# Loading the projection weights of a decoder layer in pairs of units

## The reference

```python
mod = (silu(c) @ w_ada + b_ada)                    # 2048 x 12288 weights: six parts
h = rmsnorm(x, g_pre_mix) * (1.0 + sc1) + sh1
proj = h @ w_in                                    # 2048 x 6160: q, k, v | GLA q, k, v, r | gate
o_sb = stick_breaking_attention(q, k, v)           # prompt; samples also read 64 cached pages of K and V
o_g  = gated_linear_attention(q_g, k_g, v_g, log_alpha, state) * silu(r_g)
m = concat(norm(o_sb), norm(o_g)) @ w_out          # 2048 x 2048
x = x + gt1 * rmsnorm(m, g_post_mix)
h = rmsnorm(x, g_pre_ffn) * (1.0 + sc2) + sh2
f = (silu(h @ w_ffn_gate) * (h @ w_ffn_up)) @ w_ffn_down
y = x + gt2 * rmsnorm(f, g_post_ffn)
```

## Time and profile before

| | us |
|---|---|
| median of 3 runs | 1502.29 (1501.54 to 1504.39) |
| the profiled execution | 1500.96 |
| its span in the trace | 1499.2 |
| slots 0 to 127 (first unit's matmul to the last) | about 99 to 685 |
| FFN and end | about 707 to 1499 |

### The profile page before, as it was taken

The page is one execution under the profiler, slowest core; times in us unless marked ns, Lnnn a source line. Parts: engine busy times, 40 slices in busy tenths (PEclk is TensorE's granted clock), DMA queues, the critical chain, the costliest instruction groups (busy, mean ns, idle before and its releaser), DMA issues.

```text
span 1499.2 us, 29221 instructions
## 1 busy us (share of the span) xinstructions
PE 1431.8 (96%) x11274; PEld 1272.5 (85%) x11274; DVE 913.4 (61%) x1501; ACT 661.2 (44%) x1277; POOL 105.3 (7%) x205
## 2 busy tenths in 40 slices
PE   6779999999799999998999999999999999999997
PEld 2247787887577787796899999999999999999997
DVE  2143588995777656457656666566665665446444
ACT  1023477777556553336443434434344343334333
POOL 1000311113322200100000000000000000200000
PEclk9979999999999999999999999999999999999999
DMA  9999999999999978987765565655666656855552
GB/s 369 421 341 357 391 392 405 376 333 399 401 381 332 337 261 276 400 317 268 255 187 178 167 194 178 184 177 167 191 181 182 180 170 186 236 181 182 178 179 93
DMA packets 139043, 396.54 MB, mean 265 GB/s; under 512 B 13131, under 2 KB 17394, under 8 KB 126146
## 3 DMA queue, kind: packets, MB, share of 16 engines
q1 hardware_dynamic: 117730, 319.39, 62.6%
q0 software_dynamic: 21232, 76.10, 13.4%
HBM read 382.14 MB, written 11.21 MB: 262 GB/s over the span
## 4 chain that ended last, share of the span: by engine, by line
PE 83%; DMA 10%; DVE 3%; ACT 2%; issue 1%; POOLq 0%; POOL 0%; SPq 0%; DVEq 0%; ACTq 0%
PE ps L1907 24%; PE ps L1908 24%; PE ps L1909 24%; DMA ada_s<-in_w_ada 5%; PE ps L1841 4%; DMA v_page<-in_cache_v 2%; DMA k_page<-in_cache_k 2%; PE ps L2039 2%; PE ps L1965 1%; DMA ada_r<-in_w_ada 1%; ACT k_page L780 0%; DVE k_page L1275 0%; PE ps L2068 0%; ACT w_hi L702 0%; PE ps L2060 0%
## 5 line engine op out<-in xcount | busy, mean ns | idle before, releaser
L1907 PE MATMUL ps<-h_hi,w_hi 128*128 128x264 f32 x2304 | 665.9, 289 | 6.2 <-DVE h_lo L1213 3.6
L1908 PE MATMUL ps<-h_lo,w_hi 128*128 128x264 f32 x2304 | 656.7, 285 | 0.0
L1909 PE MATMUL ps<-h_hi,w_lo 128*128 128x264 f32 x2304 | 656.2, 285 | 0.0
L1907 PEld LDWEIGHTS ps<-h_hi,w_hi 128*128 128x128 f32 x2304 | 436.1, 189 | 51.2 <-issue 36.9
L1729 DVE TENSOR_TENSOR w_lo<-raw,w_hi 128x1024 fp32r<-128x1024 f32 x256 | 309.5, 1214 | 275.5 <-ACT w_hi L1018 274.1
L1018 ACT ACTIVATE w_hi<-raw 128x1024 fp32r<-128x1024 f32 x264 | 278.4, 1059 | 405.0 <-PE ps L1909 391.2
L1908 PEld LDWEIGHTS ps<-h_lo,w_hi 128*128 128x128 f32 x2304 | 435.5, 189 | 0.1
L1909 PEld LDWEIGHTS ps<-h_hi,w_lo 128*128 128x128 f32 x2304 | 434.4, 189 | 0.0
L1225 DVE TENSOR_TENSOR w_lo<-raw,w_hi 128x1024 fp32r<-128x1024 f32 x136 | 166.2, 1223 | 151.1 <-ACT w_hi L702 143.8
L702 ACT ACTIVATE w_hi<-raw 128x1024 fp32r<-128x1024 f32 x128 | 134.9, 1055 | 182.6 <-PE ps L1909 161.8
L1908 PE MATMUL ps<-act_lo,w_hi 128*128 (+1 forms) x704 | 200.4, 285 | 0.0
(11 more groups left out here) (336 smaller groups left out, 1205.5 us busy)
## 6 DMA issues: line engine op xcount, KB each, us to landing
ada_r<-in_w_ada SPq DMA_DIRECT2D x64, 1024.0 KB, 9.5
raw<-in_w_in SPq DMA_DIRECT2D x96, 512.0 KB, 8.9
raw<-in_w_ffn_gate SPq DMA_DIRECT2D x88, 512.0 KB, 3.7
raw<-in_w_ffn_up SPq DMA_DIRECT2D x88, 512.0 KB, 3.9
raw<-in_w_ffn_down SPq DMA_DIRECT2D x88, 512.0 KB, 4.5
ada_s<-in_w_ada SPq DMA_DIRECT2D x32, 1024.0 KB, 13.7
k_page<-in_cache_k POOLq DMA_DIRECT2D x64, 512.0 KB, 8.1
v_page<-in_cache_v POOLq DMA_DIRECT2D x38, 512.0 KB, 8.1
```

What stands on the lines that cost most here:

```text
L1907: mm(out, w_hi, xh, start=first, stop=False)
L1908: mm(out, w_hi, xl, start=False, stop=False)
L1909: return mm(out, w_lo, xh, start=False, stop=last)
```

## The change

Two neighbouring units, an even and an odd one, are loaded by one transfer of 1 MB into two neighbouring places of `RAW`. The pair has one semaphore of two (`pair_in`) in place of one of four; `hi` of either unit waits for the whole pair. The pair (u, u+1) is issued where the odd unit was issued, at the odd slots, once DVE has split unit u - 3; so the even unit's issue moves one slot later, behind the `ada_load` or `state_load` of the even slot. At the start, pairs (0,1) and (2,3) are issued where units 0 to 3 were, and pair (4,5) where unit 5 was. In slot 2 nothing is loaded before the wait for `x_moved`.

Two semaphores more are needed and three are given back: `kft_ready` and `sfin_ready` become counts 1 and 2 of `gla_copied`, and `vs_copied` becomes counts 2 and 3 of `vsmp_ready`, with the same instructions as signallers and the same ones waiting. The bytes moved and the arithmetic are the same.

```diff
--- before.py
+++ after.py
@@ -253,12 +253,12 @@
         W_DOWN = W_FFN + 2 * NFF * UPC
         NSLOT = W_FFN
 
-        def unit_src(u):
+        def pair_src(u):
             g, j = divmod(u, UPC)
             if g < NIN:
-                return win_v[:, 2 * j:2 * j + 2, IN_COL[g]:IN_COL[g] + CG]
+                return win_v[:, 2 * j:2 * j + 4, IN_COL[g]:IN_COL[g] + CG]
             kp = (j + 4) % UPC
-            return wout_v[:, 2 * kp:2 * kp + 2, (g - NIN) * CG:(g - NIN) * CG + CG]
+            return wout_v[:, 2 * kp:2 * kp + 4, (g - NIN) * CG:(g - NIN) * CG + CG]
 
         def unit_dst(g, m):
             return PROJ[:, IN_DST[g] + m, :] if g < NIN else MT_[:, (g - NIN) * MT + m, :]
@@ -305,6 +305,7 @@
 
         c_in, x_in, vec_in, misc_in = sem("c_in"), sem("x_in"), sem("vec_in"), sem("misc_in")
         raw_in = sems("raw_in", 4)
+        pair_in = sems("pair_in", 2)
         ads_in = sems("ads_in", 6)
         ada_in = sems("ada_in", 9)
         kpage_in = sems("kpage_in", 5)
@@ -329,7 +330,7 @@
         k_mul, k_even, k_odd = sem("k_mul"), sem("k_even"), sem("k_odd")
         t_diff, t_exp, t_mul, t_mm, t_mask = sem("t_diff"), sem("t_exp"), sem("t_mul"), sem("t_mm"), sem("t_mask")
         att_cross, pick_ready = sem("att_cross"), sem("pick_ready")
-        kft_tr, kft_ready, g_st, sfin_ready, g_o, g_oev = sem("kft_tr"), sem("kft_ready"), sem("g_st"), sem("sfin_ready"), sem("g_o"), sem("g_oev")
+        kft_tr, gla_copied, g_st, g_o, g_oev = sem("kft_tr"), sem("gla_copied"), sem("g_st"), sem("g_o"), sem("g_oev")
         vg_tr, vg_ready, vsmp_ready = sem("vg_tr"), sem("vg_ready"), sem("vsmp_ready")
         km_ready, qz_ready = sem("km_ready"), sem("qz_ready")
         dec_mm, dec_taken = sem("dec_mm"), sem("dec_taken")
...
@@ -388,7 +389,8 @@
             sp.dma_start(PT[:, :], page_table.rearrange("b n -> (b n)").unsqueeze(0)).then_inc(misc_in, 16)
 
             def w_load(u):
-                sp.dma_start(RAW[:, u % 4, :].rearrange("p (k n) -> p k n", k=2), unit_src(u)).then_inc(raw_in[u % 4], 16)
+                sp.dma_start(RAW[:, u % 4:u % 4 + 2, :].rearrange("p s (k n) -> p (s k) n", k=2), pair_src(u))\
+                    .then_inc(pair_in[u // 2 % 2], 16)
 
             def ada_load(n):
                 p = ADA_PLACE[n]
@@ -399,13 +401,12 @@
             for n in range(6, 2 * KC):
                 sp.wait_ge(ads_used, n - 5)
                 sp.dma_start(ADS[n % 6][:, :], ada_start(n)).then_inc(ads_in[n % 6], 16)
-            for u in range(4):
+            for u in (0, 2):
                 w_load(u)
 
             sp.dma_start(WG[:, :, :], win_v[:, :, NIN * CG:NIN * CG + RANK]).then_inc(misc_in, 16)
-            for u in range(4, 6):
-                sp.wait_ge(lo_ready, u - 3)
-                w_load(u)
+            sp.wait_ge(lo_ready, 2)
+            w_load(4)
 
             sp.wait_ge(ads_used, 2 * KC)
             sp.wait_ge(tr_done, 2 + KC)
@@ -425,7 +426,8 @@
 
             for s in range(2, NSLOT - 4):
                 sp.wait_ge(lo_ready, s + 1)
-                w_load(s + 4)
+                if s % 2:
+                    w_load(s + 3)
                 if s == 2:
                     sp.wait_ge(x_free, 1)
                     sp.wait_ge(x_moved, 16)
...
@@ -696,7 +698,7 @@
                 s.activation((MROW0 if q < 4 else MROW1)[:, :], ps[:, TURN_BANK[q], :], ACT.Copy).then_inc(modrow, 1)
 
             def hi(u):
-                act.wait_ge(raw_in[u % 4], 16 * (u // 4 + 1))
+                act.wait_ge(pair_in[u // 2 % 2], 16 * (u // 4 + 1))
                 if u >= 4:
                     act.wait_ge(unit_used, u - 3)
                 s.activation(HI[:, u % 4, :], RAW[:, u % 4, :], ACT.Copy).then_inc(hi_ready, 1)
...
@@ -1567,7 +1569,7 @@
                     ins.then_inc(norm_sq, 1)
                 if st == 90:
                     dve.wait_ge(bank_out, 44)
-                    v.tensor_copy(VSMP[:, 0:4, :], PV[:, :, TP:T]).then_inc(vs_copied, 1)
+                    v.tensor_copy(VSMP[:, 0:4, :], PV[:, :, TP:T]).then_inc(vsmp_ready, 1)
                 if st == 91:
                     dve.wait_ge(norm_sum, 1)
                     rstd_of(rstd[0:64, :], rvar[0:64, :], ps[0:64, 4, 0:T], 1, 2)
...
```

More of the change, by code:

```diff
@@ L341, in stickbreak_gla_layer @@
         tok_tr, kt_ready, vt_ready = sem("tok_tr"), sem("kt_ready"), sem("vt_ready")
-        row_tr, row_ready, vs_copied = sem("row_tr"), sem("row_ready"), sem("vs_copied")
+        row_tr, row_ready = sem("row_tr"), sem("row_ready")
         norm_sq, norm_sum, norm_rs, norm_bc, norm_h = sem("norm_sq"), sem("norm_sum"), sem("norm_rs"), sem("norm_bc"), sem("norm_h")
@@ L615, in _ @@
                 if s == 56:
-                    pool.wait_ge(sfin_ready, 1)
+                    pool.wait_ge(gla_copied, 2)
                     pool.dma_start(new_state_prompt[0, 0].rearrange("h k v -> k h v"), SFIN[:, :, :]).then_inc(sfin_out, 16)
@@ L728, in evac_frees @@
                     act.wait_ge(tok_tr, 6)
-                    act.wait_ge(vs_copied, 1)
+                    act.wait_ge(vsmp_ready, 2)
                 if g == 12:
@@ L928, in _ @@
                         ins = s.activation(KFT[:, j * 512:j * 512 + 512], ps[:, 5 + j, :], ACT.Copy)
-                    ins.then_inc(kft_ready, 1)
+                    ins.then_inc(gla_copied, 1)
                 if st == 56:
@@ L935, in _ @@
                         ins = s.activation(SFIN[:, 2 * j:2 * j + 2, :].rearrange("p h v -> p (h v)"), ps[:, 5 + j, :], ACT.Copy)
-                    ins.then_inc(sfin_ready, 1)
+                    ins.then_inc(gla_copied, 1)
                 if st in (58, 59):
@@ L1015, in hi_n @@
             def hi_n(nb, u):
-                act.wait_ge(raw_in[u % 4], nb * 4 + (64 // 4 * (u // 4) + 16))
+                act.wait_ge(raw_in[u % 4], nb * 4 + (64 // 4 * (u // 4) + 16 - 4 * W_FFN))
                 act.wait_ge(unit_used, nb + (u - 3))
@@ L1592, in slot @@
                     dve.wait_ge(bank_out, 48)
-                    v.tensor_copy(VSMP[:, 4:8, :], PV[:, :, TP:T]).then_inc(vs_copied, 1)
+                    v.tensor_copy(VSMP[:, 4:8, :], PV[:, :, TP:T]).then_inc(vsmp_ready, 1)
                 if st == 98:
@@ L2080, in gla_values @@
                 if h < 2:
-                    pe.wait_ge(sfin_ready, 1)
+                    pe.wait_ge(gla_copied, 2)
                 else:
@@ L2188, in _ @@
                 if st == 55:
-                    pe.wait_ge(kft_ready, 1)
+                    pe.wait_ge(gla_copied, 1)
                     pe.wait_ge(vg_ready, 4)
@@ L2310, in _ @@
                     pe.wait_ge(norm_h, GH + 8)
-                    pe.wait_ge(vs_copied, 2)
+                    pe.wait_ge(vsmp_ready, 3)
                     pe.wait_ge(row_ready, 1)
```

## The result

Six runs of each kernel on one chip gave a median of 1510.68 us after (1507.61 to 1513.35) and 1502.37 us before (1501.54 to 1504.39). The ratio is 1.0056, with an interval of 1.0046 to 1.0066. So it became slower by 8.3 us, where 11.7 was forecast. The execution that was profiled after is the shortest of its six, 1507.61 with a span of 1506.0.

A forecast was written before the change was run, and what follows sets the result against it. PE, busy 96% of the span, was taken as the bound. Terms 3.7 + 2.3 + 5.8 - 1.4 + 2.3 - 1 = 11.7 on the profiled 1500.96 gave 1512.7, and 1.3 more for the median 1514.0 us; range 1500 to 1520.

The forecast's parts named there:

- place 1: Unit 6, slot 3: pair (6,7) lands at 129.8, PE starts unit 6 3.7 us later, slow clock adds 2.3.
- place 2: Unit 34, slot 31: late pair delays ACT's PSUM copies, so group 4 starts 5.8 us later, slow clock adds 2.3.
- given back at 240.98: Even slot's modulation block goes ahead of the even unit, so PE's 1.36 us wait at 240.98 goes: -1.4 us.
- V pages: Weights following a slot later let V pages land sooner or later: -1 us, between -1.3 and +1.3.
- Removed issues and merged semaphores: 64 fewer issues on SP, hidden behind PE's matmuls, and merged semaphores with the same signallers and waiters: 0 us.
- Rival (e): Faster by size: 0.4 us saved per unit shortens waits for DMA: 1496 us, chance 0.05.
- Units 36 to 41 land late too, but PE is by then later: After the group 4 stall PE is 4.4 us later and its reserve is back, so these cost 0.
- rival (d): Faster by order: modulation blocks and pages go ahead of weights, giving 1.4 and 5 us: 1496, chance 0.08.
- Rival (b): Lateness repeats after 240: a further group's bank copies wait, 5.8 us more: 1520, chance 0.10.
- (a): Only one of the two places, unit 6 or unit 34, bites: 6.0 or 6.7 us kept, about 1508, chance 0.15.
- (c): The room suffices everywhere, since ACT waited for PE 74 times and for landings 6: 1502, chance 0.12.
- 2.55 leaves the clock alone: PE idle 2.55 us in 402 to 406 kept clock 1.00; used in setting unit 6's clock loss at 2.3 us.

The follow-up runs named there:

- p_start: Kernel before, with pairs only for units 0 to 31 and single units for the rest, merged semaphores kept: 1504.2 against 1502.02 us, 1.0017.
- only_34: Kernel before, with one pair alone, units 34 and 35, and merged semaphores kept: 1507.02 against 1502.54 us, 1.003.
- p_tree: Kernel before, with pairs only for units 32 to 47, single units elsewhere, merged semaphores kept: 1506.32 against 1502.02 us, 1.0024.
- order_only: Kernel before, single units, merged semaphores; in even slots 28 to 56 the modulation block is issued ahead of the unit: 1505.28 against 1501.72 us, 1.0026.
- p_pages: Kernel before, with pairs only for units 48 to 95, single units elsewhere, merged semaphores kept: 1503.44 against 1502.02 us, 1.0011.
- merges: Kernel before with only the merged semaphores, no pairs, all units loaded singly: 1501.5 against 1501.72 us, 1.0001.
- late_two: Changed kernel, but each pair goes as two 512 KB transfers with a semaphore each, both issued at the odd unit: 1509.38 against 1501.72 us before, 1.0053.
- but_32_34: Changed kernel with all pairs except (32,33) and (34,35), which are single as before: 1512.83 against 1502.54 us for the kernel before, 1.0074.
- evac_first: Changed kernel with all pairs, but in slot 31 ACT frees the PSUM banks before `hi(34)`: 1510.18 against 1501.72 us for the kernel before, 1.0064.
- only_32: Kernel before, with one pair alone, units 32 and 33, and merged semaphores kept: 1504.36 against 1502.54 us, 1.0012.
- order_32: Kernel before, single units, merged semaphores; in slot 32 alone the modulation block is issued ahead of unit 36: 1505.24 against 1502.54 us, 1.0022.

## Why the prediction came out as it did

| step | predicted us | kernel after, profiled | alone, median |
|---|---|---|---|
| place 1, with its clock | 3.7 + 2.3 | 0.9 + 0 | p_start 2.2 |
| place 2, with its clock | 5.8 + 2.3 | 3.7 + 1.6 | only_34 4.5, p_tree 4.3, both less what is given back |
| given back at 240.98 | -1.4 | -1.4 | the reordering by itself: order_only +3.6 |
| V pages | -1 | +2.9 | p_pages +1.4 |

**Removed issues and merged semaphores, 0: right.** merges shows it for the semaphores. late_two puts the removed issues back and takes the size and the common semaphore away, and it comes out at 1.0053 beside 1.0056. So the three together are worth nothing that can be measured; that a gain by size and a loss by the common semaphore cancel in them isn't excluded. The Trainium skill's rule in DMA: Bandwidth & Descriptors, section Bandwidth, to batch to 1 MiB or more, would have made late_two the slower of the two; no such difference was measured. The 2.0 us per DMA that the prediction took from the same page of the Trainium skill, section Anatomy of one DMA, stand there for DMAs issued by GpSimd, and these units are issued by SP. Putting 64 issues back cost nothing that can be measured. Rival (e) has no support.

**Place 1: the mechanism was right, the term 3.7 + 2.3 was mis-sized.** PE does wait for `w_lo` at 128, but 0.5 us. Two readings failed. I took the landing of units 7 and 8 for that of the pair: the second of them landed 128.5 - 124.4 = 4.1 us behind the block ahead of it, while the pair landed at 125.7, and 2.7 us behind its block, which landed 7.1 us after its issue at 115.9, at 123.0. And I put SP's release 1.3 us later for the shifted queue; it came at 115.50, 1.5 us earlier than at 117.03. Part of the 1.5 is that execution's head start; in but_32_34, which had none, SP's release came at 117.32, 0.3 us later than before. The wait was then too short to touch the clock, which was granted in full from 124 to 136. "What it lands with" should have been the bytes behind the block, 1.3 us per 512 KB, which I had in the earlier trace rows. It isn't the single transfer that made the difference to the 4.1: in late_two the two units went out as two transfers and the second still landed 3.1 us behind its block.

**Place 2: the mechanism was right, the term 5.8 was too large, and the two late units 32 and 34 share it.** For unit 34 alone the profiled execution of only_34 meets the sum closely. It starts group 4 at 239.96, where I had 239.3, and its units after the vanished wait end 6.6 us later, where I had 5.8 + 2.3 - 1.4 = 6.7. That closeness is partly luck: the execution is the second longest of its ten, and by the median the pair costs 4.5. In the kernel after the pair landed at 233.4 and not 235.4, which took off 2 us. ACT and DVE fall behind at unit 32 and free the K pages' places later: POOL issued no page between 223.19 and 230.17, where it had issued at 226.95 and 229.03 before, and at 224.52 and 228.30 in only_34, whose pair landed at 236.1.

```profile
...
230.17 0.53 POOL L570 DMA_DIRECT2D k_page<-in_cache_k  x1 [6.45 <-ACT k_page L782]
...
```

Less traffic beside the pair would explain the 2 us; the issue times are shown, their effect on the landing is argued. The step that I missed is the unit before: I looked at `hi(8g + 10)` alone, as the copy right before the bank copies, and not at what a late unit two slots earlier does to DVE, whose page sums the bank copies also stand behind. evac_first and only_32 show that second chain.

**"Units 36 to 41 land late too, but PE is by then later": right, and more fragile than I wrote.** It is only the first stall that hides the next one; but_32_34 takes the first away and the second appears, at a higher price in the profiled execution. The intervals overlap, so that this kernel is slower than all pairs, and not just as slow, isn't shown; why it would be stays open.

**Given back, -1.4: right in the trace, wrong as a gain of its own.** The wait goes, and the same reordering puts 1 MB ahead of units that ACT and DVE need on time. order_only and order_32 lose 3.6 and 2.7 us with it. This is also what rival (d) rested on, so (d) would have lost by its own mechanism.

**V pages, -1: too low, and the size stays open.** In the profiled execution the sum of waits stayed, 12.8 to 12.7. I priced microseconds of waiting and left their pattern alone; the half-speed work behind them rose from 4.5 to 10.1 us. That arithmetic, 5.0 against 2.3, covers 2.7 of the 2.9 us of this one execution. It isn't a cost that the pairs there are shown to make: runs with single units in that stretch lost from -1.4 to 4.5 us in it, and p_pages, 1.4 by the median and -0.3 to 3.8 by its interval, can't be told from none. That interval leaves out my -1.

So the sum was 3.4 us too high in the median. By the medians place 1 was too high by 3.8 (6.0 against 2.2), place 2 with what is given back by 2.4 (6.7 against 4.3), and the V pages too low by 2.4; that the total lies no further off is partly luck, since these errors cancel in part. The sign and the chief place stood. Rival (b), a further group's bank copies, didn't happen; (a), one place, is in effect what the profiled execution shows, plus the V pages. (c) missed since the reserve of PE isn't the reserve of what stands behind `hi` on ACT.

## What to carry to other kernels

When transfers are joined, ask first which of them now starts later, and try just that: the later issue alone made all of the loss here, and the size made none that could be measured. Then follow a late tile through the order of each engine that reads it, and price what is queued behind that reader, not the tile: a deep buffer ahead of PE doesn't protect a PSUM copy that ACT can reach only after the late copy. And where engines have little slack (before, from 219 to 235.4 us, DVE was busy 14.3 of 16.4 us and ACT 11.3), don't add up or remove single stalls, since the first one hides the next. Before reading a term off one profile, see how much the same stretch moves in runs that don't touch it: for the V pages it was more than the term.

## What the runs showed that I had not expected

- One pair, the only one in only_34, made PE idle for 7.93 us and put 6.8 us of the timeline (236.9 to 243.7) at a granted clock of 0.50, 1.2 GHz.
- Much the same idle can leave the clock alone or halve it. After 2.16 us of idle at 362.88 the granted clock was 0.51 for 3.5 us; before, after 2.55 us of idle at 405.8, it had stayed at 1.00 from 405 to 409. In merges, with 2.48 us of idle at the same place, it fell to 0.51 from 405.1 to 408.5. The step "2.55 leaves the clock alone" rested on one case, and such a row should be read as one outcome of two.

The rows of the kernel before, and of merges, PE's timeline and then the stretch in the columns of the earlier trace rows:

```profile
...
405.80 0.64 PE L2039 MATMUL ps<-v_page,a_dec 128*32 128x512 f32 x4 [2.55 <-DMA v_page<-in_cache_v]
...
405.00:409.00 4.00, 3.21 (x26) 2.40 (x27) 4.00 (x21) 1.81 (x13) 0.53 (x1) 1.00 1.03 402
...
```

```profile
...
405.48 1.93 PE L2065 MATMUL ps<-v_page,a_dec 128*32 128x512 f32 x8 [2.48 <-DMA v_page<-in_cache_v]
...
405.10:408.50 3.40, 3.02 (x13) 1.39 (x14) 3.40 (x21) 1.46 (x10) 0.00 (x0) 0.51 1.04 405
...
```
